# Two transformer blocks on one core: level scores by pairs of heads, the first norm's squares summed in a tree, early loads and feed-forward splits in another order

## The reference

```python
# first block
h = rms_norm(x, norm_mix_pre_g)
proj = h @ w_in                    # q, k, v of two attentions, two gates
...
x = x + rms_norm(merged @ w_out, norm_mix_post_g)
h = rms_norm(x, norm_ffn_pre_g)
f = (silu(h @ w_gate) * (h @ w_up)) @ w_down
x = x + rms_norm(f, norm_ffn_post_g)
# second block, linear attention, per head and chunk
b = cumsum(log_a)
decay = exp(where(causal, b[i] - b[j], -inf))
scores = einsum('ik,jk,ijk->ij', q, k, decay)
o = (q * exp(b)) @ state + scores @ v
state = state * exp(b_last)[:, None] + (k * exp(b_last - b)).T @ v
```

## Time and profile before

| | us |
|---|---|
| three runs, median (lowest to highest) | 1408.23 (1407.65 to 1408.25) |
| the profiled execution | 1408.23 |
| its span in the trace | 1406.4 |
| PE busy | 1378.3 (98%) |
| DVE busy | 887.6 (63%) |
| ACT busy | 584.9 (42%) |
| POOL busy | 71.2 (5%) |
| L638, all units, six groups of matmuls | 62% of the chain that ended last |

### The profile page before, as it was taken

How to read it: one execution, slowest core, us unless ns; L and a number is a source line. 1 busy time by engine, 2 the same in 40 slices (tenths; PEclk the granted TensorE clock), 3 DMA queues, 4 the chain that set the end, 5 groups by cost and what they waited for, 6 DMA issues and landing times.

```text
span 1406.4 us, 18896 instructions
## 1 busy us (share of the span) xinstructions
PE 1378.3 (98%) x6612; PEld 1107.4 (79%) x6612; DVE 887.6 (63%) x1484; ACT 584.9 (42%) x978; POOL 71.2 (5%) x128
## 2 busy tenths in 40 slices
PE   7999999999999999999997999999999999999999
PEld 5877777778988888888884788767798888888887
DVE  5666666678777777774336777866566666565221
ACT  5455545553553333223223524566445444443111
POOL 4000000000001211220000000000000000000000
PEclk9999999999999999999998999999999999999999
DMA  5321222213225555554431211111122232323332
GB/s 188 105 75 61 75 67 74 85 61 120 86 76 180 197 192 191 193 194 156 140 127 51 74 57 65 69 62 61 60 72 90 89 104 89 104 89 116 94 97 86
DMA packets 42613, 146.80 MB, mean 104 GB/s; under 512 B 5424, under 2 KB 5696, under 8 KB 42560
## 3 DMA queue, kind: packets, MB, share of 16 engines
q1 hardware_dynamic: 34736, 120.39, 26.1%
q0 software_dynamic: 7824, 25.70, 5.5%
HBM read 143.97 MB, written 2.10 MB: 104 GB/s over the span
## 4 chain that ended last, share of the span: by engine, by line
PE 94%; DVE 4%; ACT 1%; issue 0%; DMA 0%; SPq 0%; ACTq 0%; DVEq 0%
PE bank L638 62%; PE bank L835 13%; PE bank L656 4%; PE bank L779 2%; PE bank L857 2%; PE bank L876 2%; PE bank L1070 2%; PE bank L949 2%; PE bank L894 1%; PE bank L746 1%; DVE w_lo L1815 1%; PE bank L733 1%; PE bank L897 1%; DVE y_lo L1890 1%; DVE gate_a L2017 0%
## 5 line engine op out<-in xcount | busy, mean ns | idle before, releaser
L1815 DVE TENSOR_TENSOR w_lo<-raw,w_hi 128x1024 fp32r<-128x1024 f32 (+1 forms) x224 | 270.6, 1209 | 159.6 <-ACT w_hi L1240 154.8
L1240 ACT ACTIVATE w_hi<-raw 128x1024 fp32r<-128x1024 f32 (+1 forms) x224 | 232.1, 1037 | 290.2 <-PE bank L638 262.2
L638 PE MATMUL bank<-h_hi,w_hi 128*128 128x512 f32 x856 | 338.9, 396 | 1.5 <-DVE w_lo L1815 1.5
L638 PE MATMUL bank<-h_hi,w_lo 128*128 128x512 f32 x856 | 333.4, 390 | 0.0
L638 PE MATMUL bank<-h_lo,w_hi 128*128 128x512 f32 x856 | 333.4, 389 | 0.0
L638 PEld LDWEIGHTS bank<-h_hi,w_hi 128*128 128x128 f32 x856 | 160.7, 188 | 42.0 <-issue 7.4
L638 PEld LDWEIGHTS bank<-h_hi,w_lo 128*128 128x128 f32 x856 | 160.7, 188 | 33.8
L638 PEld LDWEIGHTS bank<-h_lo,w_hi 128*128 128x128 f32 x856 | 160.8, 188 | 33.2 <-issue 1.0
L638 PE MATMUL bank<-f_hi,w_lo 128*128 128x512 f32 x352 | 136.9, 389 | 0.0
L638 PE MATMUL bank<-f_hi,w_hi 128*128 128x512 f32 x352 | 136.9, 389 | 0.0
L638 PE MATMUL bank<-f_lo,w_hi 128*128 128x512 f32 x352 | 136.9, 389 | 0.0
(11 more groups left out here) (349 smaller groups left out, 1985.2 us busy)
## 6 DMA issues: line engine op xcount, KB each, us to landing
raw<-in_w_up SPq DMA_DIRECT2D x66, 512.0 KB, 3.2
ada<-in_w_ada POOLq DMA_DIRECT2D x96, 256.0 KB, 3.1
raw<-in_w_mix SPq DMA_DIRECT2D x47, 512.0 KB, 3.2
raw<-in_w_down SPq DMA_DIRECT2D x32, 512.0 KB, 3.5
raw<-in_w_in SPq DMA_DIRECT2D x25, 512.0 KB, 3.2
raw<-in_w_gate SPq DMA_DIRECT2D x22, 512.0 KB, 3.2
raw<-in_w_out SPq DMA_DIRECT2D x16, 512.0 KB, 3.2
raw<-in_w_down SPq DMA_DIRECT2D x16, 384.0 KB, 3.5
```

The source lines that it names most:

```text
L638: last = pe.matmul(to[:, :], wt[:, slot, k, :], act_[:, rhs0 + k, :], start=(k == first and n == 0), stop=(k == K - 1 and n == 2))
L1240: act.activation(w_hi[:, s, k0:K, :], raw[:, s, k0:K, :], ACT.Copy).then_inc(hi_ready[s], 1)
L1815: dve.tensor_tensor(w_lo[:, s, k0:K, :], raw[:, s, k0:K, :], w_hi[:, s, k0:K, :].bitcast(F32), ALU.subtract).then_inc(split_ready[s], 1)
```

## The change

1. **Level scores.** PE goes through pairs of heads (0 and 1, then 2 and 3), and within a pair chunk by chunk, with the two heads in turn. The wait for the pair's two banks is one wait.
2. **First norm's squares.** ACT squares the 8 tiles into 8 places of `gate_b`, which is not in use yet; no ring, no wait. POOL's 8 adds, its clearing of `sqacc` and their semaphores are gone. DVE adds in a tree of three instructions (2048, 1024, 512 columns). On DVE the third unit's `split_lo` moves ahead of the last two `scaled_lo`, on ACT its `split_hi` ahead of the last two `scaled_hi`.
3. **First loads.** The first half of the first weights is issued from ACT's queue, as ACT's first instruction; SP issues the third unit's weights in front of the last two tiles of x.
4. **First feed-forward.** On DVE both `add_half` of the second half move up, on ACT the square of tile 7, on PE the second half's sum goes behind step 4 instead of 5. The fourth unit's split is done in halves, PE starts with the first and takes five rows of weights before the sum, not three. The next split of slot 0 moves ahead of the first silu, on ACT and DVE; the silu of the modulation's condition moves ahead of the second gated column.

```diff
-SECOND_SUM_AT = (5, 6)
+SECOND_SUM_AT = (4, 6)
...
-            for k in range(KD):
-                pool.wait_ge(sq_g[k % 2], w.next(sq_g[k % 2]))
-                pool.tensor_tensor(sqacc[:, :], sqacc[:, :], sq[:, k % 2, :], ALU.add).then_inc(sq_used[k % 2], 1)
-                pool.wait_ge(sq_used[k % 2], w.next(sq_used[k % 2]))
...
             sp.dma_start(xT[:, 0:1, :], a["x"][:, 0:1, :]).then_inc(first_x_in, 16)
-            sp.dma_start(raw[:, 0, 0:4, :], tile("w_mix", 0, 0, 4).rearrange("p (k c) -> p k c", c=P)).then_inc(first_half_in, 16)
             sp.dma_start(xT[:, 1:2, :], a["x"][:, 1:2, :]).then_inc(x_in[0], 16)
             load(0, tile("w_mix", 0, 4, KU), 4, KU)
             x_load(2)
             mix_load(1)
             x_load(4)
+            mix_load(2)
             x_load(6)
...
-            for g in range(2):
-                w.skip(sq_g[g], 4)
-                pe.wait_ge(sq_used[g], w.next(sq_used[g], times=4))
+            pe.wait_ge(first_sum, 1)
             pe.matmul(T1[:, :], ones[:, :], sqacc[:, :], start=True, stop=True).then_inc(ms_ready, 1)
...
                     three_units_by_halves(0, (T0, O0, O1))
-                    unit(S0, 0, h_hi, h_lo, 0, 3)
+                    pe.wait_ge(half_lo, 1)
+                    products(S0, 0, h_hi, h_lo, 0, 4, ready=half_lo)
+                    pe.wait_ge(split_ready[0], w.next(split_ready[0]))
+                    unit(S0, 0, h_hi, h_lo, 4, 5)
                     pe.wait_ge(x_sum, 1)
                     pe.matmul(S1[:, :], ones[:, :], sqacc[:, :], start=True, stop=True).then_inc(ms_ready, 1)
-                    unit(S0, 0, h_hi, h_lo, 3, KU)
+                    unit(S0, 0, h_hi, h_lo, 5, KU)
...
-                    for h in range(4):
-                        half = slice(64 * (h % 2), 64 * (h % 2) + 64)
+                    for t in range(2):
                         if lv >= 1:
-                            pe.wait_ge(lev_read, w.next(lev_read))
+                            pe.wait_ge(lev_read, w.next(lev_read, times=2))
                         for c in range(NCH):
                             cc = slice(P * c, P * c + P)
-                            k_of = gk[half, h // 2, cc] if lv == 0 else lev[half, lv % 2, h // 2, cc]
-                            q_of = gq[half, h // 2, cc] if lv == 0 else lev[half, lv % 2, h // 2, cc]
-                            last = pe.matmul(head_bank[h][:, cc], k_of, q_of, start=True, stop=True)
-                        last.then_inc(lev_done, 1)
+                            for m in range(2):
+                                half = slice(64 * m, 64 * m + 64)
+                                k_of = gk[half, t, cc] if lv == 0 else lev[half, lv % 2, t, cc]
+                                q_of = gq[half, t, cc] if lv == 0 else lev[half, lv % 2, t, cc]
+                                last = pe.matmul(head_bank[2 * t + m][:, cc], k_of, q_of, start=True, stop=True)
+                                if c == NCH - 1:
+                                    last.then_inc(lev_done, 1)
...
+            def x_square(k):
+
+                act.activation(gate_b[:, k, :], xT[:, k, :], ACT.Square).then_inc(first_sq, 1)
+
+            act.dma_start(raw[:, 0, 0:4, :], a["w_mix"][0:1, :, 0:4 * P].rearrange("t p n -> (t p) n")
+                          .rearrange("p (k c) -> p k c", c=P)).then_inc(first_half_in, 16)
             act.preload_act_table_set("natural_log_exp_and_others")
...
             split_hi(1)
+            second_half_square(7)
             rounded_pair(0, 2)
             x_squares(0, 1)
-            second_half_square(7)
...
-            split_hi(0)
+            split_hi(0, by_halves=1)
             split_hi(1)
             inverse_rms(buffered=False, sums=S1)
             act.preload_act_table_set("silu_and_others")
+            split_hi(0)
...
             gated(0, gate_pre, up=False, next_gate=False)
-            gated(1, gate_pre, up=False)
             act.wait_ge(cond_in, w.next(cond_in))
             act.activation(cond[:, :], cond[:, :], ACT.Silu).then_inc(cond_r, 1)
+            gated(1, gate_pre, up=False, next_gate=False)
...
+            dve.wait_ge(first_sq, KD)
+            then(dve.tensor_tensor(gate_b[:, 0:4, :], gate_b[:, 0:4, :], gate_b[:, 4:8, :], ALU.add))
+            then(dve.tensor_tensor(gate_b[:, 0:2, :], gate_b[:, 0:2, :], gate_b[:, 2:4, :], ALU.add))
+            dve.tensor_tensor(sqacc[:, :], gate_b[:, 0, :], gate_b[:, 1, :], ALU.add).then_inc(first_sum, 1)
             dve.wait_ge(lam_in, w.next(lam_in))
...
             pair_rest(0, 1)
+            add_half(0, 5, 1)
+            add_half(0, 6, 1)
             pair_scaled(0, 2)
...
             pair_scaled(0, 3)
-            add_half(0, 5, 1)
             pair_to_x(0, 3)
-            add_half(0, 6, 1)
...
-            split_lo(0)
+            split_lo(0, by_halves=1)
             then(dve.tensor_tensor(x_sq[:, 0:2, :], x_sq[:, 0:2, :], x_sq[:, 2:4, :], ALU.add))
...
             then(dve.tensor_tensor(cval[:, :], O0[:, :], rstd[:, :], ALU.mult))
+            split_lo(0)
             dve.wait_ge(silu_r, w.next(silu_r))
...
                 if second:
                     then(dve.tensor_tensor(cval[:, :], O1[:, :], rstd[:, :], ALU.mult))
-                    split_lo(0)
```

36 lines of the change are left out of this document (17 added, 19 removed).

## The result

The changed kernel takes 1399.52 us (median of four runs, 1399.37 to 1399.82), the kernel before 1407.94 in the same comparison: ratio 0.9938, 95% interval 0.9926 to 0.9949. The forecast was 1400.4, in a range from 1398.4 to 1402.6. The profiled execution took 1399.48 with a span of 1397.8, 8.6 less than before.

A forecast was written before the change was run, and what follows sets the result against it. TensorE was taken as the bound, 94% of the chain that ended last. Level scores -5.4, stall -1.53, first load -0.37 and feed-forward -0.55 sum to -7.85 us, from 1408.23 to 1400.4, range 1398.4 to 1402.6.

The forecast's parts named there:

- Levels: Level scores: blocks of 32 products fall from 2.75 to 1.97 us, 0.78 less in seven rounds, -5.4 us.
- the eighth block gains nothing: Last level: a VectorE chain holds the transposes, so TensorE arrives 0.78 us earlier and waits 0.78 longer.
- The stall: TensorE's wait before the third unit, for its weights' remainder: goes once GpSimd's adds no longer slow VectorE, -1.53 us.
- The first load: First weights issued from ScalarE's queue: first matmul at 7.45, the middle of 6.4 and 8.5, -0.37 us.
- rival (a): Start: first weights and x's first tile compete, first matmul at 8.5 instead of 7.45, total 1401.4; chance 0.27.
- the forecast's two terms: Start: -1.53 us for TensorE's wait before the third unit and -0.37 us for the earlier first weights.
- Feed-forward: First feed-forward: shorter wait for the fourth unit's split, less new waits, -0.55 us in sum, bounds -1.0 and +0.4.
- Split in halves: First feed-forward, fourth unit: TensorE starts on the first half of slot 0's split, at 407.1 instead of 408.18, -1.0 us.
- the moved additions: First feed-forward: two earlier adds delay slot 1's split by 0.8 us; the sum's move gives nearly all back, +0.07.
- the split two units on: First feed-forward: slot 0's split before the first silu delays slot 1's next split, which TensorE waits for, +0.35 us.
- The slower rival, (d): Level scores: alternation removes the heads' overlap, block 3.64 us instead of 2.75, +7.1 us, total 1412.9; chance 0.03.

The follow-up runs named there:

- the experiment that takes the wait away: The changed kernel with VectorE's product with the keys ahead of the last two picks and state copies ahead of the gain: 1398.4 us, ratio 0.9928.
- the levels alone: The kernel before with only the level scores of two heads issued in turn: 1402.65 us against 1408.17, ratio 0.9963.
- the feed-forward alone: The kernel before with only the first feed-forward's changes: 1407.98 us against 1408.17, ratio 0.9999.
- the trace with 13: The changed kernel with the third unit's split back behind all eight scaled tiles on VectorE and ScalarE: 1400.1 us, ratio 0.9943.

## Why the prediction was right, and where not

**Levels, the term that carried it: right.** The block was put at 1.97 from the step of one place (0.111) and the hand-over of the column halves; it is 1.99, and pairs in one half take 3.43, near the 3.64 worked out for 32 in a row. Seven rounds at 0.78 were to give 5.4; the trace gives 5.45, alone 5.5. That the eighth block gains nothing is shown by the 0.81 of wait in front of the transposes, forecast as 0.78, and by the experiment that takes the wait away.

**The stall: right in cause, its size from one execution.** GpSimd's additions doubled VectorE's instructions (with them back they double again), and without them the old order makes no stall either. But the new order alone removed it too: with the additions back the third unit still starts without a wait, and what they cost there is a late sum and what follows it. In these traces the stall needed both, the additions and the old order. (With 6 slow steps and not 8, TensorE would have asked 0.4 earlier there and waited about 0.2, an estimate from its rows.) The 1.53 (1.37 of it idle) was read in an execution with 12 slow first matmuls; with 6 of them TensorE was idle for 2.24 and 2.23 us at the same place. The squares were to end at 18.6, the sum at 22.8: 18.4 and 22.7.

**The first load: wrong.** The step that failed is the -0.37 us, the middle between 6.4 and 8.5 for the first matmul. In the ten traces with the load on ScalarE's queue the weights land at 4.1 to 4.5 instead of 6.0 to 6.7, but x's first tile at 5.0 to 6.2 instead of 4.3 to 5.8; rounding x and rounding and splitting the weights then follow each other on ScalarE. The seven of them that changed nothing in front of the first matmul have it at 7.4 to 8.5, 7.87 on average; the four with the load on SyncE's queue at 7.7 to 8.2, 7.94. So the load's place is worth about 0.1 us on average, less than such small groups can tell from nothing. In all eight traces with the load on ScalarE's queue and x's tile rounded first, the first matmul comes 2.33 us after that tile has landed, whenever the weights came: the early weights wait, and the forecast's 7.45 would have needed x's tile at 5.12. The 8.5 of rival (a) came once in the seven.

**What the sum left out.** The first matmuls are 0.43 apart, the step of the 1.2 GHz level, and the prediction did not speak of them. That number differs between executions: in the traces of before, of the levels alone and of the feed-forward alone there are 12, 6 and 6 such steps, after the change 6, and in six others with the same start 6, 7, 13, 8, 6 and 11. Each costs 0.20 us. The granted clock of the page reads 1.00 there, so only the steps show it. The Trainium skill (TensorE: Matmul & The Clock Gate, Part 1, What's actually happening) says that this count changes from run to run of the same kernel; the trace agrees. In the kernel before the stall hides it: the third unit began at 22.96, 23.05 and 23.16 with 12, 6 and 6 slow steps, because VectorE set the time. After the change nothing hides it, and the number of slow steps goes through to the third unit. So the start gave 2.86 in the profiled pair, 1.53 of the stall, 0.16 of the first matmul and 1.17 of slow steps, but 1.8 in the trace with 13 (its third unit begins at 21.16), where the forecast's two terms make 1.90. The forecast's sum is 7.85 us and the medians differ by 8.42; the 0.6 between them is of the size of a few slow steps, and less than the interval of the ratio (1.6 us to each side) can tell. That the sum came so near is in part luck: the number of slow steps could have moved it by over a microsecond, and 0.37 of it rested on a gain that was hardly there.

**Feed-forward: right.** Split in halves -0.95 (forecast -1.0), the moved additions +0.72 and -0.72 (forecast +0.8 and nearly all of it back), the split two units on +0.33 (forecast +0.35): -0.62 for -0.55. What gave the 0.72 back is the wait of 0.75 at 396.99, which the forecast did not name. By time alone none of this could be shown.

**Lost in between:** 0.31 us between the feed-forward and the levels was not foreseen. The two lists place it: the first matmul behind the second block's first norm (772.70 before) comes 3.56 earlier, the one at 778.46 only 3.21. Between them stand 11 steps of 0.43 before and 13 after the change. Their number differs between the other traces too (6 with the levels alone), and no run was made to tell what sets it.

The slower rival, (d), needed heads that wait for one another. A block came near its 3.64 only where heads of the same half were paired: 3.43, and 1411.0 where it had 1412.9.

## What to carry to other kernels

In this kernel, products of 64 rows gained when they were issued so that neighbours lie in different halves of the rows. To find such a place, compare a block's length with the number of instructions times the step, and look what the last block of such a chain waits for. GpSimd's additions were not free beside VectorE: they doubled its two-input instructions, so a few more on VectorE can be cheaper. And a stall of TensorE hides variations ahead of it: when it goes, what it hid shows in the time.

## What was not expected of the hardware

- With eleven products that compute nothing in the idle time at the start, the six slow steps of the first matmuls were gone and the third unit began 1.25 us earlier. These products stayed at a slow step (0.21) to their last instruction, and the work behind them was fast.
- Two stalls of TensorE, of 2.23 and 1.85 us, were followed by matmuls at a granted clock of one half, which cost 1.6 and 1.8 us more; stalls of 1.37 and 2.24 us in other traces were not. What decides between them was not tried.
